# Normalised tiles of a hybrid decoder layer transposed by DMA instead of TensorE, with the first MLP norms taken before the mixer's end and the MLP weights loaded by one queue

## The chip, the cores and the metric

The kernel runs on the 8 cores of one Trainium2 chip. Each core works by itself on its share of the batch; nothing is exchanged. A core has five engines, each with its own instruction stream that runs in program order: TensorE (PE: matmuls, and transposes written as matmuls), VectorE (DVE), ScalarE (ACT), GpSimd (POOL) and SyncE (SP). PE writes to PSUM, eight banks of 128 x 512 float32; the other operands lie in SBUF. SP, ACT and POOL also issue DMA transfers, each in its own order. The metric is the device time of the slowest core, in microseconds (us).

## The reference

One layer of a decoder with adaptive norms: a token mixer (recurrence on half the width, short convolution on the other) and an MLP, each with a residual, then a final norm. Cut to what matters:

```python
D_MODEL = 1024; BATCH = 8; SEQ = 2048; DEC_BATCH = 128; DEC_SEQ = 8; H_REC = 4; D_FF = 4096

def hybrid_layer(x, c, s_rec, s_conv, lb, w_ada, b_ada, w_in, w_conv, g_onorm, w_out, w_up, w_down):
    mod = jax.nn.silu(c) @ w_ada + b_ada
    sh1, sc1, g1, sh2, sc2, g2 = jnp.split(mod[:, None, :], 6, axis=-1)
    h = rms_norm(x) * (1 + sc1) + sh1
    q, fz, i, g, gb, gc, hv = jnp.split(h @ w_in, SPLITS, axis=-1)
    logf = jnp.log(lb_h + (1.0 - lb_h) * jax.nn.sigmoid(fz32))
    k = (1.0 - lb_h) * jax.nn.sigmoid(-fz32)
    o_rec, s_rec_new = hgrn2_chunked(q, k, logf, i, s_rec)      # state 128 x 128 per head, in chunks
    o_rec = per_head_rms(o_rec) * g_onorm * jax.nn.silu(g)
    y_conv, s_conv_new = short_conv(gc * hv, s_conv, w_conv)
    mix = jnp.concatenate([o_rec, gb * y_conv], axis=-1) @ w_out
    x = x + g1 * mix
    h2 = rms_norm(x) * (1 + sc2) + sh2
    x = x + g2 * (jnp.square(jax.nn.relu(h2 @ w_up)) @ w_down)
    return x, s_rec_new, s_conv_new

def reference(...):        # one layer, for 8 prompts and for 128 samples with a state of their own
    ...
    y = rms_norm(x) * g_final
```

## The kernel before

**Work of a core.** One prompt of 2048 tokens, in 16 blocks of 128, and 16 sample sequences of 8 tokens, which make one more block. The mixer takes the prompt in eight tiles of two blocks, p0 to p7, with the sample tile s after p3: the order is p0, p1 (their steps interleaved), p2, p3, s, p4, p5, p6, p7. Then the MLP takes the 17 blocks in six groups: (sample, 0, 1), (2, 3, 4), (5, 6, 7), (8, 9, 10), (11, 12, 13), (14, 15).

**The order.** The program is written down as a list of operations with what they read and write. A planner takes the list with its place in it as priority and with a cost for each operation, and puts each engine's operations in a fixed order; semaphores are set by what depends on what. So an operation's place on its engine is decided before the run, and an engine stands at an instruction whose operand is not there.

**A norm.** `normed` loads a block x (128 tokens x 1024, ACT's queue) into one of two buffers `xn`, forms the sum of squares and the factor on ACT (Square, Ln, Exp), and DVE writes x times the factor as bf16 into one of two buffers, W0 and W1. The matmuls want the width on the partitions, so each block is transposed, in eight pieces of 128 x 128. PE does this (`tr`, L415) into a PSUM bank, M1 (ring `NR`); DVE reads the bank and writes scale and shift applied: `hT` for the mixer (`norm1`, eight passes of 128 x 256 a tile; two buffers, a third early), `h2T` for the MLP (`norm2`, eight passes of 128 x 128 a block). For the sample block, which has another scale and shift for each sequence, `sample_mod` does it with four tensor-tensor passes of 128 x 512.

**A mixer tile.** `mixer_tile` runs in steps: F (decays), V (values), Q (queries), G (gate), R (the recurrence, block by block: transpose of the keys `nk`, scores, masked scores `sm` times values, state products, each with the one bank M0, ring `MR`; then the norm of the output: square, a reduction by a matmul with ones into M0, Ln, Exp, a DVE product, two POOL products into `mix`), C, H and B (convolution, matmuls of `hT` with the blocks of w_in), and then the output projection (wout, banks U0 and U1) with the residual. `norm1` of the next tile stands in the list ahead of a tile's own steps. For the sample tile SP loads 16 states `Sl` and stores them back, in seven buffers.

**Around the MLP.** At step B of p7 the seven first loads of up weights (`wup`, SP's queue, out of a bf16 copy in DRAM, `wscr`) and `norm2` of the first group are listed. `h2T` lies over the buffers W6 to W8 that the steps up to B use, `wup` over w_in, `wdn` partly over what the mixer leaves; so each waits for the last use. Down weights go through POOL's queue, held back by `load_dn` until an up load has landed. Per group the list has `up` (256 matmuls of up to 384 columns for three blocks, square of relu into `uT`), `norm2` of the next group, `down` (192 matmuls of 512 columns, the second residual, final norm, store).

In the rows a name ends in a buffer number of the tool's own (`W_135`, `W_136` are W0, W1; `hT_60` to `hT_62` are hT0 to hT2). Helpers: matmul L404, transpose L415, activation L431, tensor-tensor L438, tensor-scalar L442 and L444, DMA L465.

Of the kernel before, what the change touches and what calls it, by code (L numbers as in the profile page):

```python
# [368 lines left out]
def build_program():  # L369
# [348 lines left out]
    def normed(src_d, rdeps):  # L718
        x, xn = xnR.take()
# [5 lines left out]
        return nbv, nbn  # L725

    def sample_mod(nbv, nbn, dst, dst_n, c0, j_sh, j_sc):
        M, Mn = NR.take()
        Mb = M[:, :].bitcast(BF16)
        tr([(Mb[:, j * 128:(j + 1) * 128], nbv[:, j * 128:(j + 1) * 128], ident) for j in range(8)], [nbn, "cB"], [Mn])  # L730
        for jh in range(2):
            W, Wn = WT.take()
# [484 lines left out]
```

How the kernel before makes its waits and increments, by code:

```python
            def run(e, h):  # L325
                for o in order[e]:
                    for key, (val, d) in need_of[o.idx].items():
                        if d.chan is not None:
                            h.wait_ge(csem[key], val * 16)
                        else:
                            h.wait_ge(esem[key], d.cnt)
                    ins = o.fn(h)
                    if o.chan is not None:
                        ins.then_inc(csem[o.chan], 16)
                    elif o.signal:
                        ins.then_inc(esem[e], 1)
                if e == "sp":
                    for c, n in self.chans.items():
                        h.wait_ge(csem[c], n * 16)
```

## Time and profile before

| | us |
|---|---|
| median of 3 runs (lowest to highest) | 929.19 (928.15 to 932.9) |
| the profiled execution | 927.96 |
| its span, slowest core (5) | 926.4 |
| busy: PE, DVE, ACT, POOL | 826.0, 466.9, 366.2, 166.8 |
| PE's share of the chain that ended last | 75% |

The profile is of one execution. A row of the stage view gives start and end of a stretch, its length, then for PE, PE's weight loads (PEld), DVE, ACT and POOL the time that the engine worked in it with the number of instructions, then the granted clock of PE as a share of full speed, the busy share of the 16 DMA engines, and GB/s. A row of a timeline gives start, duration, engine, line, operation, out<-in with shapes, how many like it follow one another, and in square brackets how long the engine stood before it and what released it. A row of the view by lines gives, behind the bar, busy time in all and mean ns of one, then the idle time before. A row of transfers gives queue, count, KB each and the median us from issue to landing. Matmuls are pipelined: the distance between two starts says more than a duration.

The run has three parts: about 75 us of loading and modulation, the mixer until 437, the MLP from 437 to 916.

### The profile page before, as it was taken

To read this page: it belongs to the slowest core of one execution; us is meant where nothing else is said; L and a number is where in the kernel's file an instruction comes from. 1 tells how busy PE (TensorE), PEld (TensorE's weight loads), DVE (VectorE), ACT (ScalarE), POOL (GpSimd) and SP (SyncE) were. 2 spreads that over 40 slices of the span, in tenths; PEclk is the share of its full clock that TensorE was granted. 3 is DMA by queue.
4 is the path that set the end of the run, shared out by engine and by line. 5 is a ranking of instruction groups with operands and counts; after the bars stand their busy time and mean duration, and the time that the engine had idled before them with its cause. 6 is when DMAs were issued, how large, how long until landed. Compare 5 with 4: busy or idle time off the path is not lost.

```text
span 926.4 us, 16715 instructions; the slowest of 8 cores (914.6 to 926.4 us)
## 1 busy us (share of the span) xinstructions
PE 826.0 (89%) x5929; PEld 513.6 (55%) x5929; DVE 466.9 (50%) x851; ACT 366.2 (40%) x780; POOL 166.8 (18%) x218
## 2 busy tenths in 40 slices
PE   0147999999898999986999999999999999999995
PEld 0124876777676657653654565456446545644862
DVE  0023597667879687685443445234514533442421
ACT  2036558374747567632330333133214312311411
POOL 2000022332153342242201200200120021002001
PEclk9997999999999999996999999999999999999998
DMA  8999789999346668798996211210221012002001
GB/s 161 215 183 196 137 161 162 201 181 235 112 149 239 140 174 201 188 241 187 227 195 157 95 43 47 91 69 2 91 69 46 24 46 91 2 1 83 31 2 45
DMA packets 27436, 113.93 MB, mean 123 GB/s; under 512 B 3845, under 2 KB 4229, under 8 KB 22362
## 3 DMA queue, kind: packets, MB, share of 16 engines
q0 software_dynamic: 4848, 39.19, 26.8%
q1 hardware_dynamic: 17610, 55.85, 18.9%
q10 hardware_dynamic: 4896, 17.83, 6.2%
q8 instruction: 48, 0.79, 0.3%
q14 instruction: 34, 0.28, 0.1%
HBM read 129.56 MB, written 30.88 MB: 173 GB/s over the span
## 4 chain that ended last, share of the span: by engine, by line
PE 75%; DVE 6%; DMA 6%; issue 6%; ACT 5%; ACTq 0%; POOL 0%; DVEq 0%; POOLq 0%
PE G L404 41%; PE U L404 23%; PE O L404 9%; DMA win_44<-w_in 5%; PE M L415 1%; DMA cB<-constB 1%; ACT W_140 L431 1%; DVE Sd_85 L438 1%; DVE h2T L444 1%; PE M L404 1%; DVE Ts_84 L438 1%; ACT Sb_86 L431 1%; ACT W_142 L431 0%; ACT W_141 L431 0%; ACT W_139 L431 0%
## 5 line engine op out<-in xcount | busy, mean ns | idle before, releaser
L444 DVE TENSOR_SCALAR h2T<-M,modT 128x128 bf16<-128x128 bf16 x128 | 43.9, 343 | 23.7 <-PE M L415 13.7
L431 ACT ACTIVATE W_140<-G 128x384 f32<-128x384 f32 (+2 forms) x38 | 19.7, 519 | 52.3 <-PE G L404 52.3
L415 PE MATMUL M<-cB,W_135 128*128 128x128 bf16 (+1 forms) x144 | 13.3, 231 | 30.1 <-DVE lnoml L438 20.9
L431 ACT ACTIVATE W_135<-xn_145 128x1024 bf16<-128x1024 f32 x17 | 17.9, 1053 | 45.6 <-PE M L415 36.2
L431 ACT ACTIVATE W_136<-xn_146 128x1024 bf16<-128x1024 f32 x17 | 17.9, 1053 | 25.7 <-PE M L415 15.8
L438 POOL TENSOR_TENSOR xr_147<-xr_147,W_138 128x512 f32<-128x512 f32 x8 | 10.5, 1312 | 97.1 <-DVE W_138 L438 96.9
L415 PEld LDWEIGHTS M<-cB,W_135 128*128 128x128 bf16 (+1 forms) x144 | 9.9, 104 | 32.6 <-issue 31.2
L431 ACT ACTIVATE Sb_86<-Sd_85 128x512 bf16<-128x512 f32 x16 | 10.0, 627 | 37.8 <-DVE Sd_85 L438 37.8
L438 POOL TENSOR_TENSOR xr_147<-xr_147,W_137 128x512 f32<-128x512 f32 x5 | 6.3, 1267 | 102.6 <-DVE W_137 L438 102.6
L438 DVE TENSOR_TENSOR uT<-W_138,G 128x384 bf16<-128x384 f32 (+1 forms) x26 | 13.7, 528 | 17.2 <-ACT W_138 L431 16.6
L404 PE MATMUL G<-hT_60,win_44 128*128 128x256 bf16 x128 | 18.4, 303 | 4.4 <-DMA win_44<-w_in 4.4
L431 ACT ACTIVATE W_137<-G 128x384 f32<-128x384 f32 (+1 forms) x24 | 11.4, 475 | 25.8 <-PE G L404 25.0
L438 DVE TENSOR_TENSOR Ts_84<-Sd_85,U 128x512 f32<-128x512 f32 x31 | 21.1, 682 | 0.7
L431 ACT ACTIVATE W_140<-W_140 128x512 f32<-128x512 f32 x32 | 20.1, 630 | 2.1
L404 PE MATMUL G<-wdn_129,uT 128*128 128x512 bf16 x88 | 20.8, 379 | 0.0
L404 PE MATMUL G<-wdn_128,uT 128*128 128x512 bf16 x88 | 20.8, 379 | 0.0
L404 PE MATMUL G<-wdn_127,uT 128*128 128x512 bf16 x88 | 20.8, 379 | 0.0
L404 PE MATMUL G<-wdn_130,uT 128*128 128x512 bf16 x88 | 20.8, 379 | 0.0
L438 DVE TENSOR_TENSOR uT<-W_137,G 128x384 bf16<-128x384 f32 (+1 forms) x24 | 12.9, 537 | 15.6 <-ACT W_137 L431 14.1
L431 ACT ACTIVATE W_138<-G 128x384 f32<-128x384 f32 (+1 forms) x26 | 12.2, 469 | 21.0 <-PE G L404 21.0
L438 DVE TENSOR_TENSOR uT<-W_139,G 128x384 bf16<-128x384 f32 (+1 forms) x24 | 13.0, 542 | 14.5 <-ACT W_139 L431 14.5
L438 DVE TENSOR_TENSOR W_138<-U,Gp 128x512 f32<-128x512 f32 x16 | 11.0, 687 | 16.3 <-PE U L404 15.0
(565 smaller groups left out, 2149.0 us busy)
## 6 DMA issues: line engine op xcount, KB each, us to landing
wscr<-w_up POOLq DMA_DIRECT2D x8, 1024.0 KB, 14.9
xn_146<-x ACTq DMA_DIRECT2D x9, 512.0 KB, 4.7
xn_145<-xp ACTq DMA_DIRECT2D x8, 512.0 KB, 11.0
xn_146<-xp ACTq DMA_DIRECT2D x8, 512.0 KB, 9.6
ada_111<-w_ada POOLq DMA_DIRECT2D x4, 1024.0 KB, 13.4
ada_112<-w_ada POOLq DMA_DIRECT2D x4, 1024.0 KB, 22.5
xn_145<-x ACTq DMA_DIRECT2D x8, 512.0 KB, 3.4
xr_148<-xp SPq DMA_DIRECT2D x6, 512.0 KB, 14.7
```

The costliest lines, as they stand in the source:

```text
L404: ins = e.matmul(o_, lhsT=l_, rhs=r_, start=st, stop=sp_, skip_group_check=True)
L415: ins = e.transpose(out=o_, in_=i_, identity=id_)
L431: return P.op("act", lambda e: e.activation(out=out, in_=in_, func=func, **kw), r, w, c, prio=prio)
L438: return P.op(eng, lambda e: e.tensor_tensor(out=out, in0=in0, in1=in1, op=op), r, w, vec_cost(eng, out, mode), prio=prio)
L444: f = lambda e: e.tensor_scalar(out=out, in0=in0, scalar1=s1, scalar2=s2, op0=op0, op1=op1)
```

## The change

- From the fourth prompt tile on (`ti > 2`), for the sample tile and for all MLP norms, the normalised block is transposed by a DMA from SP's queue (`turned`): out of W0 or W1 into the `xn` buffer that held x. These are 28 transfers of 256 KB. DVE reads SBUF then; `norm1` has 16 passes of 128 x 128 a tile in place of 8 of 128 x 256. Tiles p0 to p2 keep the transposes on PE.
- `NR` is gone; M0 and M1 both serve the recurrence, and the transposes of p0 to p2.
- The three norms of the first MLP group are listed at step C of p7, up to and with their transposes (the third into the gate buffer `Gs`); at step B `norm2` gets them and only writes `h2T`.
- Up weights load through POOL's queue, in front of the down weights, which no longer wait for an up load.
- Modulation of the second half and the gates move: from tile 2's step Q to its R, from 2's B to tile 3's F, from 3's Q to 3's R.

```diff
-    GA = BankRing(["G0", "G1", "G2"]); MR = BankRing(["M0"]); NR = BankRing(["M1"]); ...
+    GA = BankRing(["G0", "G1", "G2"]); MR = BankRing(["M0", "M1"]); ...
     def load_up(j):
-        up_ops[j] = dma("sp", flat(wup[j]), wscr_d[j], ["wscr%d" % j], [wup_n[j]], MB2 / 2)
+        up_ops[j] = dma("pool", flat(wup[j]), wscr_d[j], ["wscr%d" % j], [wup_n[j]], MB2 / 2)
     def load_dn(j):
-        gate = up_ops.get(4 if j == 2 else 7)
-        dma("pool", flat(wdn[j]), wdn_d[j], [], [wdn_n[j]], MB2, after=[gate] if gate else ())
+        dma("pool", flat(wdn[j]), wdn_d[j], [], [wdn_n[j]], MB2)
...
+    def turned(nb):
+        nbv, nbn, x, xn = nb
+        xt = x[:].bitcast(BF16)[:, 0:1024].rearrange("p (j t) -> p j t", t=128)
+        P.op("sp", lambda e: e.dma_start_transpose(xt, nbv.rearrange("p (j n) -> p j n", n=128)), [nbn], [xn], 1200.0, dma=300000.0)
+        return xt, xn
...
     def norm1(kind, ti):
+        if ti > 2:
+            for b in range(2):
+                xt, xn = turned(nbs[b])
+                for jj in range(8):
+                    ts("dve", h[:, jj, b * 128:(b + 1) * 128], xt[:, jj, :], modT[:, 8 + jj, 0:1], modT[:, jj, 0:1], ...)
+            return h, hn
         for jh in range(2):
-            M, Mn = NR.take()
+            M, Mn = MR.take()
...
-    def norm2(blocks):
+    def norm2(blocks, ready=None):
         for s, blk in enumerate(blocks):
-            nbv, nbn = normed(x1_d[blk], ["x1_%d" % blk])
+            xt, xn = ready[s] if ready else turned(normed(x1_d[blk], ["x1_%d" % blk]))
...
-            M, Mn = NR.take()
-            tr([(Mb[:, j * 128:(j + 1) * 128], nbv[:, j * 128:(j + 1) * 128], ident) for j in range(8)], [nbn, "cB"], [Mn])
...
+            if step == "C" and n_ + 1 == len(tiles):
+                n0 = [turned(normed(x1_d[b], ["x1_%d" % b], (Gs, "Gs") if i == 2 else None)) for i, b in enumerate(bgroups[0])]
             if step == "B" and n_ + 1 == len(tiles):
                 for j in UPORD[:7]:
                     load_up(j)
-                norm2(bgroups[0])
+                norm2(bgroups[0], n0)
```

PE at the end of tile p7, before; names here keep their buffer and bank (G1<-hT1_61 is bank G1 from buffer hT1, wout and mix are the output projection's):

```order
L404 MATMUL G1<-hT1_61,win4_47 128x256 x8
L415 MATMUL M1<-cB_156,W1_136 128x128 x8
L404 MATMUL M0<-sq1_91,cB_156 128x512
L415 MATMUL M0<-cB_156,nk3_70 128x128 x2
L415 MATMUL M0<-cB_156,nk0_67 128x128 x2
L404 MATMUL M0<-qd3_66,nk3_70 128x128 x2
L404 MATMUL M0<-qd0_63,nk0_67 128x128 x2
L404 MATMUL U0<-vt0_74,kt1_72 128x128 x4
L404 MATMUL U1<-vt0_74,kt1_72 128x128 x4
L404 MATMUL O0<-sm0_88,vt0_74 128x128 x4
L404 MATMUL O0<-qd3_66,Sb1_87 128x64 x2
L404 MATMUL O0<-qd0_63,Sb1_87 128x64 x2
```

The same place after:

```order
L404 MATMUL G0<-hT1_61,win4_47 128x256 x8
L404 MATMUL M0<-qd3_66,nk3_70 128x128 x2
L404 MATMUL M0<-qd0_63,nk0_67 128x128 x2
L404 MATMUL G0<-hT1_61,win4_47 128x256 x8
L404 MATMUL G1<-hT1_61,win4_47 128x256 x16
L404 MATMUL O0<-sm0_88,vt0_74 128x128 x4
L404 MATMUL O0<-qd3_66,Sb1_87 128x64 x2
L404 MATMUL O0<-qd0_63,Sb1_87 128x64 x2
L404 MATMUL O0<-qd3_66,Sb0_86 128x64 x2
L404 MATMUL O0<-qd0_63,Sb0_86 128x64 x2
L404 MATMUL M1<-sq0_90,cB_156 128x512
L404 MATMUL U0<-wout0_50,mix2_152 128x512 x8
```

The L415 transposes out of W1 and W0 are gone, the key transposes (`nk`) stand further up, and the scores (`qd` with `nk`) stand ahead of the last projection's matmuls (`win4`) instead of behind them.

PE from the first group's up stage (`wup`, the last block of columns) into its down stage (`wdn`), before:

```order
L404 MATMUL G<-h2T,wup_59 128x384 x16
L415 MATMUL M<-cB,W_135 128x128 x8
L404 MATMUL G<-wdn_127,uT 128x512 x8
L404 MATMUL U<-wdn_127,uT 128x512 x16
L415 MATMUL M<-cB,W_136 128x128 x8
L404 MATMUL G<-wdn_128,uT 128x512 x8
```

and after:

```order
L404 MATMUL G<-h2T,wup_59 128x384 x16
L404 MATMUL G<-wdn_127,uT 128x512 x8
L404 MATMUL U<-wdn_127,uT 128x512 x16
L404 MATMUL G<-wdn_128,uT 128x512 x8
L404 MATMUL U<-wdn_128,uT 128x512 x16
```

The transposes of the next group's norms, eight at a time, have gone from between the matmuls.

DVE in tile p4, where `hT1` of tile p5 is written (`Sl`, `km` are the sample states and their keys), before:

```order
L438 TENSOR_TENSOR ub0_92<-WX1_114,G1 128x16x8
L438 TENSOR_TENSOR Sd0_85<-Ts0_84,dec1_99 128x512
L444 TENSOR_SCALAR hT1_61<-M1,modT_154 128x256
L448 SCALAR_TENSOR_TENSOR W8_143<-ub0_92,vecT_104,W8_143 128x128
L444 TENSOR_SCALAR hT1_61<-M1,modT_154 128x256
L448 SCALAR_TENSOR_TENSOR W8_143<-ub0_92,vecT_104,W8_143 128x128
L444 TENSOR_SCALAR hT1_61<-M1,modT_154 128x256 x2
L448 SCALAR_TENSOR_TENSOR W8_143<-ub1_93,vecT_104,W8_143 128x128 x2
L438 TENSOR_TENSOR W4_139<-O0,W4_139 128x512
```

and after, where the scaling that this block's transpose needs, `L442 TENSOR_SCALAR W0_135<-xn0_145,st4_161 128x1024`, stands three rows ahead of the first of these:

```order
L438 TENSOR_TENSOR Sl0_118<-Sl0_118,U1 128x512
L448 SCALAR_TENSOR_TENSOR W8_143<-ub1_93,vecT_104,W8_143 128x128 x2
L438 TENSOR_TENSOR mix1_83<-G2,W8_143 128x4x128
L448 SCALAR_TENSOR_TENSOR sg1_79<-G0,vecT_104,W5_140 128x256
L442 TENSOR_SCALAR km1_126<-kt2_73,cF_155 128x512
L448 SCALAR_TENSOR_TENSOR sg1_79<-G0,vecT_104,W5_140 128x256
L438 TENSOR_TENSOR Sl2_120<-Sl2_120,U1 128x512
L452 SCALAR_TENSOR_TENSOR W8_143<-cB_156,WX3_116 128x512
L438 TENSOR_TENSOR Sl1_119<-Sl1_119,U0 128x512
L442 TENSOR_SCALAR km1_126<-kt2_73,cF_155 128x512
L438 TENSOR_TENSOR qd1_64<-G1,WX2_115 128x512
L444 TENSOR_SCALAR hT1_61<-xn0_145,modT_154 128x128 x2
```

Before, the pass reads the PSUM bank M1; now it reads xn0, which the DMA writes, and 13 rows stand between the scaling and the first pass.

## Rows read from the trace of the kernel before

**Rows 1.** The stages of core 5, columns as told above.

```profile
75.00:240.00 165.00, 158.86 (x1525) 118.51 (x1523) 110.04 (x195) 95.64 (x195) 35.60 (x60) 0.97 0.91 184
240.00:410.00 170.00, 155.57 (x1371) 111.47 (x1369) 135.01 (x227) 107.80 (x215) 65.04 (x85) 0.99 0.66 174
410.00:437.00 27.00, 16.41 (x101) 8.59 (x99) 17.48 (x35) 9.37 (x21) 7.30 (x8) 0.68 1.00 202
420.00:430.00 10.00, 4.21 (x16) 1.87 (x17) 6.21 (x17) 2.18 (x7) 2.11 (x3) 0.50 0.74 134
437.00:916.00 479.00, 477.53 (x2737) 262.80 (x2735) 188.74 (x368) 131.83 (x304) 48.74 (x41) 1.00 0.25 71
```

**Rows 2.** Timeline of PE between an up stage and a down stage.

```profile
562.64 1.46 PE L404 MATMUL U<-h2T,wup_59 128*128 128x384 bf16 x8
563.94 0.61 PE L415 MATMUL M<-cB,W_136 128*128 128x128 bf16 x8
564.38 1.89 PE L404 MATMUL U<-wdn_127,uT 128*128 128x512 bf16 x8
566.11 1.89 PE L404 MATMUL U<-wdn_128,uT 128*128 128x512 bf16 x8
```

**Rows 3.** Timeline of PE from the mixer's end to the MLP.

```profile
411.08 0.61 PE L415 MATMUL M<-cB,W_136 128*128 128x128 bf16 x8
...
417.86 1.01 PE L415 MATMUL M<-cB,W_135 128*128 128x128 bf16 x8 [0.66 <-DVE W_139 L438]
...
420.80 0.59 PE L404 MATMUL M<-sq_90,cB 128*128 128x512 bf16 x1 [1.25 <-ACT st_161 L431]
423.54 1.01 PE L415 MATMUL M<-cB,W_136 128*128 128x128 bf16 x8 [2.15 <-DVE h2T L444]
427.39 3.57 PE L404 MATMUL U<-wout_50,mix_152 128*128 128x512 bf16 x8 [2.83 <-POOL mix_152 L438]
...
437.02 3.25 PE L404 MATMUL G<-h2T,wup_53 128*128 128x384 bf16 x19
```

**Rows 4.** Timelines of ACT, DVE and POOL in the same stretch.

```profile
420.08 0.58 ACT L431 ACTIVATE sq_90<-O 128x512 bf16<-128x512 f32 x1
...
424.27 0.63 ACT L431 ACTIVATE W_137<-W_137 128x512 f32<-128x512 f32 x1 [2.19 <-DVE h2T L444]
...
425.01 0.69 DVE L438 TENSOR_TENSOR W_137<-O,W_137 128x512 f32<-128x512 f32 x1 [1.61 <-ACT W_137 L431]
...
426.52 0.72 POOL L438 TENSOR_TENSOR mix_152<-W_137,sg_78 128x256 bf16<-128x256 f32 x1
```

**Rows 5.** Groups by line: DVE's passes for the norms, and a tensor-tensor pass.

```profile
L444 DVE TENSOR_SCALAR h2T<-M,modT 128x128 bf16<-128x128 bf16 x128 | 43.9, 343 | 23.7 <-PE M L415 13.7
L438 DVE TENSOR_TENSOR Ts_84<-Sd_85,U 128x512 f32<-128x512 f32 x31 | 21.1, 682 | 0.7
...
L444 DVE TENSOR_SCALAR hT_60<-M,modT 128x256 bf16<-128x256 bf16 x32 | 13.1, 409 | 3.9 <-PE M L415 2.2
```

**Rows 6.** Timeline of DVE early on: a pass of 128 x 136 in SBUF.

```profile
47.22 0.23 DVE L442 TENSOR_SCALAR modT<-modT 128x136 f32<-128x136 f32 x1
```

**Rows 7.** Transfers: issue, count, KB each, median us to landing.

```profile
wdn_134<-w_down POOLq DMA_DIRECT2D x1, 1024.0 KB, 48.5
...
Sl_120<-srec SPq DMA_DIRECT2D x2, 256.0 KB, 8.8
...
recs<-Sl_124 SPq DMA_DIRECT2D x2, 256.0 KB, 3.6
...
recp<-rout SPq DMA_DIRECT2D x1, 256.0 KB, 21.9
```

**Rows 8.** Timeline of PE at the start: p1's first projection.

```profile
78.78 3.57 PE L404 MATMUL G<-hT_62,win_44 128*128 128x256 bf16 x16 [2.79 <-DVE hT_62 L444]
```

**Rows 9.** Timelines of DVE and PE: hT1 of p5 written, and first used.

```profile
251.80 0.41 DVE L444 TENSOR_SCALAR hT_61<-M,modT 128x256 bf16<-128x256 bf16 x1
...
281.26 1.91 PE L404 MATMUL G<-hT_61,win_44 128*128 128x256 bf16 x16
```

**Rows 10.** Timeline of POOL: the issue of the last down weights.

```profile
450.99 0.57 POOL L465 DMA_DIRECT2D wdn_134<-w_down  x1
```

More of the change, by code:

```diff
@@ L716, in rstd, with normed @@
         return s_, sn
-    def normed(src_d, rdeps):
-        x, xn = xnR.take()
+    def normed(src_d, rdeps, buf=None):
+        x, xn = buf or xnR.take()
         dma("act", x[:], src_d, rdeps, [xn], 128 * 4096)
@@ L737, in sample_mod @@
             shb = AP(modT, (j_sh + 4 * jh) * 17 + 1, [[544, 128], [17, 4], [1, 16], [0, 8]])
-            tt("dve", tmv, trv, scb, ALU.mult, [Mn, "modT"], [Wn])
+            tt("dve", tmv, trv, scb, ALU.mult, [xn, "modT"], [Wn])
             tt("dve", hv, tmv, shb, ALU.add, [Wn, "modT"], [dst_n])
@@ L1007, in mixer_tile @@
             dma("sp", x1_d[xblk + b], xr[:], [xrn], ["x1_%d" % (xblk + b)], 128 * 4096)
-    def norm2(blocks):
+    def norm2(blocks, ready=None):
         for s, blk in enumerate(blocks):
-            nbv, nbn = normed(x1_d[blk], ["x1_%d" % blk])
+            xt, xn = ready[s] if ready else turned(normed(x1_d[blk], ["x1_%d" % blk]))
             if blk == SAMPLE:
-                sample_mod(nbv, nbn, h2T, "h2T%d" % s, s * 128, 16, 24)
+                sample_mod(xt, xn, h2T, "h2T%d" % s, s * 128, 16, 24)
                 continue
-            M, Mn = NR.take()
-            Mb = M[:, :].bitcast(BF16)
-            tr([(Mb[:, j * 128:(j + 1) * 128], nbv[:, j * 128:(j + 1) * 128], ident) for j in range(8)], [nbn, "cB"], [Mn])
             for j in range(8):
-                ts("dve", h2T[:, j, s * 128:(s + 1) * 128], Mb[:, j * 128:(j + 1) * 128], modT[:, 24 + j, 0:1], modT[:, 16 + j, 0:1],
-                   ALU.mult, ALU.add, [Mn, "modT"], ["h2T%d" % s], mode=1.0)
+                ts("dve", h2T[:, j, s * 128:(s + 1) * 128], xt[:, j, :], modT[:, 24 + j, 0:1], modT[:, 16 + j, 0:1],
+                   ALU.mult, ALU.add, [xn, "modT"], ["h2T%d" % s], mode=4.0)
     def up(blocks):
@@ L1127, in build_program @@
         for step in gen(n_):
-            if n_ == 2 and step == "Q":
+            where = ("2R", "3F", "3R")
+            key = "%d%s" % (n_, step)
+            if key == where[0]:
                 late_mod(0)
                 load_ada(8); load_ada(9)
-            if n_ == 2 and step == "B":
+            if key == where[1]:
                 late_mod(1)
                 load_ada(10); load_ada(11)
-            if n_ == 3 and step == "Q":
+            if key == where[2]:
                 gates(1)
+            if step == "C" and n_ + 1 == len(tiles):
+                n0 = [turned(normed(x1_d[b], ["x1_%d" % b], (Gs, "Gs") if i == 2 else None)) for i, b in enumerate(bgroups[0])]
             if step == "B" and n_ + 1 == len(tiles):
```

15 lines of the change are left out of this document (8 added, 7 removed).

## The prediction, made before the changed kernel had run

> **What bounds the kernel now.** I read the span by stages first [rows 1]: what counts is how near TensorE (PE) comes to filling each. The MLP, 437 to 916 us, is PE from end to end: 477.53 of 479 us, DMA at 0.25. An instruction taken off PE there is time taken off the kernel. The mixer from 240 to 410 is less pure: PE works 155.57 of 170 us, VectorE (DVE) 135.01, so 14.4 us of PE time go to waits, and DVE, which works in program order, has 35 us to spare (busy share 0.79). The hole is 410 to 437: PE works 16.41 of 27 us, its granted clock is 0.68 (0.50 from 420 to 430), and the DMA share is 1.00. The PE timeline of that hole [rows 3] and the rows of the other engines beside it [rows 4] say what is in it: transposes of the first MLP norms (L415, out of W_136, W_135, W_136) in between the last steps of the recurrence, each of which waits for DVE; a reduction at 420.80; and the output projection only at 427.39, which waited 2.83 us for POOL's `mix`.
>
> **The change, part by part** (against the profiled execution: 927.96 us, span 926.4, so 1.56 us lie outside the span; the median of the runs is 929.19, 1.2 above it).
>
> *E, MLP norms.* Of the 17 norm blocks 14 lie between an up and a down stage. In the MLP eight transposes start at 563.94 and the next matmul at 564.38 [rows 2]: 0.45 us a block. Nothing else is on PE then, so 14 x 0.45 = **-6.3 us**. What replaces them must hide: load, norm, DMA transpose, eight DVE passes. A group's down stage is 24 groups of eight matmuls (1.73 us each, [rows 2]) = 41.5 us for three blocks. Two buffers of x serve three blocks, so the third block's load waits for the first's DVE passes; allow 8 us for that and 4 for the third's own norm and passes, and the cover still holds for a transpose of about 29 us.
>
> *D, the transition.* PE reaches 411.08 with its last projection done and starts the output projection at 427.39: 16.3 us [rows 3]. Only a little of that is the recurrence's work: four `kt` transposes, four scores and eight state products of 128 columns (16 x 0.056) and one reduction of 512 (1.73 / 8), 1.1 us on PE, which after the change stand ahead of the last projection's matmuls. What must follow the last projection is the output of the last chunk (about 1 us with its hand-over) and a chain [rows 4]: square 0.58, reduction 0.59, Ln (taken as the Exp) 0.63, Exp 0.63, DVE 0.69, two on POOL 2 x 0.72, and five hand-overs of about 0.13 (from 420.80 plus 0.59 and from 426.52 plus 0.72 to the next start): 5.2 us. So 16.3 - (1.0 + 5.2 + 1.1) = 9.0 us saved. In the trace the chain was held by the norms: Exp at 424.27 stood behind a DVE pass of `h2T` [rows 4]. The output projection, too, took 9.63 us (427.39 to 437.02), where four groups of its kind at full clock take 4 x 1.73 = 6.9; the clock had fallen in the hole before. The hole gets shorter but stays; I take half of 2.7: -1.4. The three norms themselves now run earlier, at step C, with three loads, three squares on ACT and three scalings on DVE, into a stage where DVE has 0.21 to spare. The writing of `h2T` must still wait for step B (the space is shared); it is 16 passes and four sample passes (0.23 and 0.68, by [rows 5, 6]), about 6 us, and hides under chain and projection (13 us). D = -9.0 - 1.4 = **-10.4 us** (bounds -6 and -13: all of the norms' 2.8 us of DVE and ACT on the path and no clock back, or the full clock back and the hand-over nil).
>
> *B, mixer tiles.* For the sample tile and tiles p3 to p7, 11 blocks of eight transposes leave PE: 11 x 0.45 = 4.9 us. Between nothing (if PE only waits longer) and all of it I take 0.6, below PE's share of 0.92, since some stand before waits: **-3.0 us**. DVE: the eight passes of 128x256 out of PSUM, 0.409 each, 3.3 us a tile [rows 5], become 16 of 128x128 out of SBUF. No such row exists; nearest are 0.343 (the same size out of PSUM, [rows 5]) and 0.23 (128x136 in SBUF, float32, [rows 6]). By 0.23 that is 3.7 us a tile, by 0.343 5.5: 0.4 to 2.2 us more on DVE a tile, in its spare time; it costs nothing or, over five tiles, 11 us if DVE were the bound. I take 0, by the SBUF row and because h is done early: p5's last pass ran at 251.80 and PE first used it at 281.26 [rows 9]. In the MLP and the hole the same passes get cheaper for DVE, which doesn't matter there.
>
> *C, the wait added.* DVE meets a tile's passes in its fixed order; if the transpose has not landed, everything behind stands: the scans, the scores' masks, the states of the sample tile, and PE behind these. In the new order the closest distances from a norm's scaling to its first pass are 13 rows of that order (second blocks of p4 and p5), 17 (both of p6), 22 or more for the rest. At 0.68 a row [rows 5] and a busy share of 0.79, 13 are 11.2 us and 17 are 14.6 us. The transpose moves 256 KB. Nearest rows [rows 7]: 256 KB transfers of the same queue and stage take 3.6 to 8.8 us; one of 256 KB issued in the hole took 21.9. I take 6, from the first two, since the transposes are issued where these run. Then C = **0**. SP also issues in order, and the second block of p5 stands behind four reloads of sample states that wait for stores; I leave that in the range (+3).
>
> *A, start.* Tiles p0 to p2 keep PE transposes, now through two banks that the recurrence shares. p1's h was waited for 2.79 us [rows 8], and its transposes no longer stand behind `kt`; on the other side a transpose of p2 now stands ahead of the first use of p1's h. I take **-1** (-4 to +3). The later gates and modulation keep the same work: 0.
>
> *Loads.* All up and down weights now go through POOL's queue. wdn_134 was issued at 451 [rows 10] and took 48.5 [rows 7], so it landed near 499.5; it was first needed near 515 (437, an up stage of 32 x 1.30, then 7/8 of the down's 41.5), and 13 us sooner, near 502, by B and D. I price this at 0.
>
> Sum: -6.3 - 10.4 - 3.0 - 1.0 = -20.7, so 927.96 - 20.7, **about 907 us**. Own range: 898 to 916.
>
> The trace has the eight PE transposes at 56 ns each [rows 2]. The Trainium skill ("VectorE: DVE Perf Modes", The three transpose paths) gives a 128x128 bf16 transpose 390 ns on TensorE and 1309 ns through the DMA's crossbar, and its Rules for kernel authors say to use TensorE where PSUM will do as the destination. The row is far under the page's TensorE figure, and no row here shows the DMA's. By the page a block would take 8 x 1.309 = 10.5 us, an estimate just inside the 11.2 above, and the sum would stand; with the wait in the queue on top it would fall under the second rival.
>
> **The rivals.**
> 1. *The hole stays.* With the norms gone, the tail hangs on DVE and ACT (state update, `Sb`, mask), which have their own three norms to do just before. For it: DVE at 0.79, and 1.25 and 2.83 us of the PE waits in the hole [rows 3] were for ACT and POOL. Against it: the Exp row [rows 4]. Then D is -3, B -1.5, A 0: -10.8, **917 us**.
> 2. *Slower: the transposes land late and DVE stands.* Mechanism C with a transpose of T us: 2 x (T - 11.2) + 2 x (T - 14.6) us are lost in the mixer, all on the path while PE has no other tile's matmuls left. The loss equals the gain of 20.7 at T = 18. At the 21.9 of [rows 7], 36 us and a few more from the blocks at 22 rows: 928 - 21 + 36 = 943; at 20, **936 us**. For it: SP's queue has the states' stores and reloads ahead, and no transpose row exists. Against it: the rows at 3.6 to 8.8.
> 3. *The first MLP starves.* One queue for 16 loads of 1 MB: `wup` come behind each other, and the hole had a DMA share of 1.00 already [rows 1]. If the last loads land 10 us later than before, near 510 where 502 is wanted, 8 are lost: **916 us**; it also takes POOL's time for issuing, beside `mix`.
> 4. *Better.* The two banks let scores and `kt` run ahead, and a third of the 14.4 us of PE waits goes, with the full clock in the projection: -27, **900 us** or a little under.
>
> **How the numbers follow.** Forecast 0.50; rival 1 0.18; rival 3 0.10; rival 2 0.14; rival 4 0.08. About 0.5% (4.6 us) is what a measurement of this kernel can tell from no change, so faster is below 924.5, slower above 933.8. The forecast, rival 4 and most of rivals 1 and 3 are faster: 0.77. What is left of these, and the mild end of rival 2, is same: 0.10. Slower is rival 2's rest: 0.13. The range leaves out rival 2 (0.14) and the far end of rival 4: 895 to 928.
>
> **What would show it.** E: no L415 between up and down, and the next up some 1.35 us sooner per group of three. D: the gap on PE between the last projection and the output projection near 7.5 us instead of 16.3, its clock above 0.50, `h2T` passes after the gated multiply. B, C: DVE's waits by releaser: none, or few, on the transposes; a landing time of 4 to 9 us. If DVE waits on them, with PE waiting for DVE in 240 to 410, rival 2 holds. Rival 3: PE waiting for a wup or wdn load between 425 and 510. The forecast is wrong at once if the transposes take more than about 15 us each, or if the stage 240 to 410 gets longer.

## The result, and the profile after

The changed kernel takes 972.12 us (median of 4 runs, 968.68 to 972.4) where the kernel before takes 929.77 (4 runs beside it): 1.0443 times as long, with an interval of 1.0406 to 1.0479. The forecast was 907, the range 895 to 928. It is slower by 42 us, and the sign is wrong.

Ratios, here and below, compare undisturbed runs alone. The profiled execution took 971.97 us. Its cores, each with its span and the mean granted clock of PE:

```profile
core 0: 915.7 us, clock 0.980
core 1: 949.0 us, clock 0.958
core 2: 930.7 us, clock 0.971
core 3: 926.4 us, clock 0.972
core 4: 954.2 us, clock 0.962
core 5: 970.1 us, clock 0.951
core 6: 937.8 us, clock 0.971
core 7: 918.0 us, clock 0.976
```

In the kernel before all eight lay between 914.6 and 926.4. So there are two things to explain: why cores 0 and 7 gain only 3.7 us each (from 919.4 and 921.7), and why the others lose up to 44. The work is the same on all eight, and in the other three executions other cores lead and trail: core 1 is the fastest in one, with 918.8 us, and the slowest in the other two, with 970.4 and 970.5. Which core loses is no property of the core.

Stages of core 5 after (columns as in [rows 1]; the third stretch is the hole before the MLP, the last two are pieces of the first):

```profile
75.00:240.00 165.00, 117.69 (x1007) 82.61 (x1006) 84.16 (x146) 73.97 (x146) 30.14 (x49) 0.87 0.98 133
240.00:465.00 225.00, 195.50 (x1747) 142.03 (x1746) 170.07 (x305) 130.59 (x263) 74.68 (x101) 0.95 0.78 177
467.00:488.00 21.00, 13.94 (x81) 7.52 (x80) 16.39 (x37) 3.64 (x7) 7.10 (x9) 0.84 1.01 239
488.00:968.00 480.00, 470.65 (x2623) 256.20 (x2620) 187.02 (x370) 134.19 (x316) 50.47 (x44) 1.00 0.33 83
140.00:150.00 10.00, 0.00 (x0) 0.00 (x0) 0.00 (x0) 0.00 (x0) 0.00 (x0) 0.50 1.70 69
...
95.00:110.00 15.00, 14.88 (x140) 11.73 (x139) 9.17 (x21) 9.20 (x21) 0.72 (x2) 1.00 1.06 174
```

Between 75 and 240 PE does 1007 matmuls where it did 1525 [rows 1]. Between 140 and 150 no engine executes anything, while the DMA engines are busy and move 69 GB/s (the share above 1 counts overlapping packets). The PE timeline names the hole:

```profile
128.45 0.49 PE L404 MATMUL G<-hT_61,win_44 128*128 128x256 bf16 x3 [0.52 <-DVE mix_83 L438]
166.31 1.25 PE L404 MATMUL G<-hT_61,win_44 128*128 128x256 bf16 x5 [37.36 <-issue]
```

PE stood 37.36 us in the middle of a group of eight equal matmuls, with nothing that the profile shows as its releaser. SP's queue on the same core just before (start, duration of the issue, transfer):

```profile
101.23 1.62 SPq L730 DMA_TRANSPOSE xn_145<-W_135  x1
102.96 23.47 SPq L730 DMA_TRANSPOSE xn_146<-W_136  x1
126.52 0.47 SPq L465 DMA_DIRECT2D gates<-xr_149  x1
175.37 0.34 SPq L465 DMA_DIRECT2D Gp<-gates  x1
```

These are the two blocks of p3, the first tile that goes by DMA. Issuing the second alone held SP for 23.47 us. The DMA view of 110 to 160 us shows what they do to the core's other transfers. First core 5 (queue: packets, MB, share of 16 engines; then transfers with the median us from issue to landing):

```profile
q1 hardware_dynamic: 1822, 0.45, 74.5%
q0 software_dynamic: 274, 1.95, 45.2%
q14 instruction: 1, 0.01, 0.0%
...
ada_112<-w_ada POOLq DMA_DIRECT2D x1, 1024.0 KB, 57.4
wout_51<-w_out POOLq DMA_DIRECT2D x1, 1024.0 KB, 53.4
...
xn_146<-W_136 SPq DMA_TRANSPOSE x1, 63.7
```

Then core 0, in the same 50 us of the same run:

```profile
q1 hardware_dynamic: 2241, 2.25, 32.2%
q8 instruction: 4, 0.07, 0.5%
...
ada_112<-w_ada POOLq DMA_DIRECT2D x1, 1024.0 KB, 9.7
wout_51<-w_out POOLq DMA_DIRECT2D x1, 1024.0 KB, 10.0
...
xn_146<-W_136 SPq DMA_TRANSPOSE x1, 14.8
```

The hardware queue of core 5 moved 0.45 MB in 1822 packets (1858 packets of all kinds were under 512 bytes) and held the 16 engines for 74.5% of the window. Weight loads that took 10 us on core 0 took 53 to 57. Queue q8, of the kind "instruction", has four packets on core 0 and none on core 5. Cores 4, 5 and 6 agree in this: q8, which has a packet of 16 KB every 10 to 20 us in the kernel before, has none there between some 108 us and 152.5, 164.0 and 146.3 us, and on each of them PE goes on 2.2 to 2.3 us after that late packet. So it looks as if PE's stand was for its own instructions, stuck in the same crowd. That rests on these rows, and was not tried alone.

The other cores follow the same pair of transfers, if not strictly. Landing time of p3's second block, and the mixer from p0's first projection matmul to the end of p7's last (before: 349.8 to 355.6 us, 352.7 in the mean):

| core | 0 | 7 | 3 | 2 | 1 | 6 | 4 | 5 |
|---|---|---|---|---|---|---|---|---|
| landing, us | 14.8 | 18.8 | 18.4 | 18.7 | 28.3 | 45.0 | 51.7 | 63.7 |
| mixer, us | 364.3 | 364.9 | 375.1 | 375.0 | 397.5 | 388.2 | 394.7 | 418.2 |

Core 1 stands out of this order because of a second late block, p6's second. It was issued into a stretch with the DMA share at 0.99 (318 to 352 us) and landed after 30.7 us; DVE stood for it before p6's passes:

```profile
319.62 1.27 SPq L730 DMA_TRANSPOSE xn_145<-W_135  x1
350.37 2.43 DVE L444 TENSOR_SCALAR hT_60<-xn_145,modT 128x128 bf16<-128x128 bf16 x6 [15.55 <-DMA xn_145<-W_135]
```

On cores 3 and 5 the same block took 22.9 and 25.1 us, and DVE stood 8.73 and 10.23 us for it; on the other five cores it took 9.4 to 11.7 us. DVE waited as well for the gate of the prompt, `Gp`: 8.2, 7.0 and 8.7 us on cores 4, 5 and 6.

The parts that were to gain did gain. The MLP takes 482.0 or 482.1 us on five of the eight cores (489.3 or 489.4 before on six), and between up and down there is nothing on PE, against [rows 2]:

```profile
611.41 1.46 PE L404 MATMUL U<-h2T,wup_59 128*128 128x384 bf16 x8
612.71 1.89 PE L404 MATMUL U<-wdn_127,uT 128*128 128x512 bf16 x8
```

The transition on core 5's PE, against [rows 3]:

```profile
467.58 2.78 PE L404 MATMUL G<-hT_61,win_47 128*128 128x256 bf16 x24
470.20 0.39 PE L404 MATMUL O<-sm_88,vt_74 128*128 128x128 bf16 x4
...
472.69 0.38 PE L404 MATMUL M<-sq_90,cB 128*128 128x512 bf16 x1 [1.86 <-ACT sq_90 L431]
478.26 3.57 PE L404 MATMUL U<-wout_50,mix_152 128*128 128x512 bf16 x8 [5.20 <-POOL mix_152 L438]
...
487.54 1.63 PE L404 MATMUL G<-h2T,wup_53 128*128 128x384 bf16 x9
```

From the end of the last projection (PE's next instruction starts at 470.20) to the output projection it is now 8.1 us, 8.0 to 8.2 over the cores (before 15.2 to 16.3). The L415 rows are gone from it; what PE waits for is the square, and then POOL's `mix`.

### The profile page after: what moved, and what is told of

Same layout as the page of the kernel before. It is cut to its first block, busy times and chain, and to the rows that moved or that the text cites. A ratio compares the mean times of both kernels' runs of the same rounds, so it can differ in the third digit from the quotient of the medians.

```text
span 970.1 us, 16398 instructions; the slowest of 8 cores (915.7 to 970.1 us)
## 1 busy us (share of the span) xinstructions
PE 821.9 (85%) x5705; PEld 506.0 (52%) x5705; DVE 475.0 (49%) x891; ACT 366.0 (38%) x780; POOL 172.3 (18%) x226
## 3 DMA queue, kind: packets, MB, share of 16 engines
q1 hardware_dynamic: 46026, 54.80, 25.5%
## 4 chain that ended last, share of the span: by engine, by line
PE 62%; DMA 16%; DVE 8%; issue 6%; ACT 3%; SPq 3%; POOL 1%; DVEq 0%; POOLq 0%; ACTq 0%
PE G L404 33%; PE U L404 21%; PE O L404 8%; DMA gates<-xr_149 5%; DMA win_44<-w_in 4%; DMA xn_145<-W_135 3%; SPq L730 3%; DMA wscr<-w_up 3%; DMA Gp<-gates 1%; DVE hT_61 L444 1%; DMA cB<-constB 1%; DVE hT_60 L444 1%; DVE W_143 L448 1%; ACT W_140 L431 1%; ACT W_142 L431 1%
## 5 line engine op out<-in xcount | busy, mean ns | idle before, releaser
L431 ACT ACTIVATE W_140<-G 128x384 f32<-128x384 f32 (+2 forms) x38 | 19.7, 519 | 85.2 <-PE G L404 66.9
L404 PE MATMUL G<-hT_61,win_44 128*128 128x256 bf16 (+1 forms) x128 | 15.7, 272 | 39.2 <-issue 37.4
L404 PEld LDWEIGHTS G<-hT_61,win_44 128*128 128x128 bf16 x128 | 11.3, 102 | 42.2 <-issue 40.3
L415 PE MATMUL M<-cB,W_135 128*128 128x128 bf16 (+1 forms) x32 | 3.4, 261 | 31.4 <-DVE lnoml L438 18.9
L431 ACT ACTIVATE W_137<-G 128x384 f32<-128x384 f32 (+1 forms) x24 | 11.4, 476 | 45.9 <-PE G L404 25.8
L438 DVE TENSOR_TENSOR sm_88<-M,cB 128x512 bf16<-128x512 f32 x9 | 6.1, 680 | 37.9 <-PE M L404 37.9
L431 ACT ACTIVATE W_135<-xn_146 128x1024 bf16<-128x1024 f32 x7 | 7.4, 1059 | 45.7 <-DVE h2T L444 28.3
L438 DVE TENSOR_TENSOR uT<-W_137,G 128x384 bf16<-128x384 f32 (+1 forms) x24 | 12.9, 537 | 22.2 <-ACT W_137 L431 20.8
L444 DVE TENSOR_SCALAR h2T<-xn_145,modT 128x128 bf16<-128x128 bf16 x64 | 22.4, 350 | 2.4 <-PE U L404 0.2
L404 PE MATMUL U<-wout_50,mix_82 128*128 128x512 bf16 x48 | 13.0, 419 | 10.3 <-DVE W_138 L438 7.6
L431 ACT ACTIVATE W_136<-xn_145 128x1024 bf16<-128x1024 f32 x7 | 7.4, 1056 | 37.0 <-DMA xn_145<-x 36.9
L431 ACT ACTIVATE W_142<-G 128x512 f32<-128x512 f32 x10 | 5.8, 584 | 40.8 <-PE G L404 40.8
## 6 DMA issues: line engine op xcount, KB each, us to landing
wscr<-w_up POOLq DMA_DIRECT2D x8, 1024.0 KB, 11.9
xn_145<-xp ACTq DMA_DIRECT2D x8, 512.0 KB, 10.4
```

The lines of the kernel that those rows point to most:

```text
L404: ins = e.matmul(o_, lhsT=l_, rhs=r_, start=st, stop=sp_, skip_group_check=True)
L415: ins = e.transpose(out=o_, in_=i_, identity=id_)
L431: return P.op("act", lambda e: e.activation(out=out, in_=in_, func=func, **kw), r, w, c, prio=prio)
L438: return P.op(eng, lambda e: e.tensor_tensor(out=out, in0=in0, in1=in1, op=op), r, w, vec_cost(eng, out, mode), prio=prio)
L444: f = lambda e: e.tensor_scalar(out=out, in0=in0, scalar1=s1, scalar2=s2, op0=op0, op1=op1)
```

## The experiments

Three theories stand in the expectations: S, that DMA transposes issued while the DMA engines are full are what costs; V, that the short DVE passes of 128 x 128 cost; O, that the moved gates, the shared banks or the single queue cost. The runs e1 to e4, e5 to e8 and e9 to e12 each had the kernel before run beside them, which took 930.16, 930.75 and 927.06 us; across these groups ratios are compared, not times.

**e1_mlp_only**: the mixer's tiles and the sample block go back to PE; the MLP norms and all else stay as changed.

```diff
-        if ti > 2:
+        if ti > 7:
...
-            xt, xn = turned(normed(xs_d[:, :], []))
+            tr([(Mb[:, j * 128:(j + 1) * 128], nb[0][:, j * 128:(j + 1) * 128], ident) for j in range(8)], [nb[1], "cB"], [Mn])
```

> All mixer tiles, the sample tile too, go back to transposes on TensorE (two banks); MLP norms stay with the DMA, the first three held ready. Theory S (DMA transposes in the stage of full DMA starve TensorE of instructions on some cores, and the slowest core counts) and theory V (80 short VectorE passes out of SBUF slow the mixer on every core) both expect the mixer of before with the shorter transition and MLP: 929 - 7.4 - 6.4, some 912 to 918 us, cores within 12 us of each other. Theory O (the two banks, the moved gates and the one queue slow the mixer by themselves) expects 935 us or more.

929.09 us, 0.9988 of before (0.9976 to 1.0). The loss goes with the mixer's transposes, which speaks for S or V; but the time is not as low as they have it, so something in the rest costs as well. It has two places. The mixer is 360.1 us in the mean of the cores (352.7 before): on all eight, DVE waits 8.7 to 14.5 us once for the gate of the prompt, where it waited 0 to 3.5 before. On core 1:

```profile
154.18 0.69 DVE L438 TENSOR_TENSOR W<-U,Gp 128x512 f32<-128x512 f32 x1 [14.54 <-DMA Gp<-gates]
```

Its load was issued at 134.18, 2.4 us later than before (131.83), so it is mainly DVE that gets there sooner. And the second MLP group is late (e6).

**e2_p3_by_pe**: only p3 goes back to PE (`if ti > 3`).

> Only tile p3 goes back to TensorE; the sample tile, p4 to p7 and the MLP stay with the DMA. Theory S expects the TensorE stalls without a releaser between 100 and 170 us to go and the slowest core to come within some 15 us of the fastest: 920 to 937 us. Theory V expects only about 3 us: 965 us or more, with the cores still 30 us and more apart.

943.61 us, 1.0149 (1.0121 to 1.0177): of the 42 us, some 28 hang on the two blocks of one tile. The spread goes with them: the mixer takes 373.4 to 381.5 us on all cores, and no core's PE stands more than 1.3 us with no releaser. What stays above before is e1's gate wait (9.0 to 14.9 us on all cores), the passes (e4, e12) and transposes that are still late: one mixer block on each core, issued at 347 to 356 us, took 10.5 to 28.9 us to land, and the first transpose of the second MLP group held SP for 36.1 to 51.8 us (MLP 490.5 to 497.0 us). How the rest divides among these was not run apart.

**e3_two_unread**: the kernel before, with two added transposes of p3's blocks that nobody reads. They stand where the change has them, and write into the x buffers; PE still makes the tile.

```diff
+        if ti == 3:
+            for (nbv, nbn), (x, xn) in zip(nbs, ((last_x[2], last_x[3]), (last_x[0], last_x[1]))):
+                xt = x[:].bitcast(BF16)[:, 0:1024].rearrange("p (j t) -> p j t", t=128)
+                P.op("sp", lambda e, nbv=nbv, xt=xt: e.dma_start_transpose(xt, nbv.rearrange("p (j n) -> p j n", n=128)), [nbn], [xn], 1200.0, dma=300000.0)
```

> The kernel before with two more DMA transposes, of p3's two normalised blocks into the buffers of x; nobody reads them, TensorE still transposes, VectorE's passes are as before. Theory S expects stalls of TensorE without a releaser, 10 to 40 us, on some cores between 100 and 170 us, a late gates transfer there, and 935 to 975 us. Theory V expects no change: 927 to 932 us.

945.66 us, 1.0168 (1.0149 to 1.0186): two transfers of 256 KB whose result is not used cost 16 us. No pass, bank or gate is changed here, so S needs neither V nor O. But the way is not the one that S expected: PE never stands more than 1.8 us without a releaser, and DVE at most 1.0 us for the gate. So this run does not show that a transpose takes PE's instructions; what a late one holds up depends on what stands behind it. Here that is visible on core 1. The transfers took 32.4 and 39.0 us to land (35.7 in the mean); the next load of x into the same buffer, on ACT's queue, has to wait for that, and ACT's work stands behind it (ACT, and ACT's queue):

```profile
116.60 0.63 ACT L431 ACTIVATE W<-W 128x512 f32<-128x512 f32 x1
137.52 0.34 ACTq L465 DMA_DIRECT2D xn<-xs  x1
137.96 0.63 ACT L431 ACTIVATE Sb<-Sd 128x512 bf16<-128x512 f32 x1 [20.73 <-DMA xn<-W]
```

Over the cores, sorted by that landing time (10.3, 12.6, 20.9, 21.6, 25.7, 32.8, 35.6, 35.7 us) the mixer takes 354.5, 356.7, 368.1, 364.7, 374.1, 376.7, 374.3 and 385.1 us: about one for one.

**e4_plain_copy**: each transpose is a plain copy of the same 256 KB, in the same place of the same queue.

```diff
-        P.op("sp", lambda e: e.dma_start_transpose(xt, nbv.rearrange("p (j n) -> p j n", n=128)), ...)
+        P.op("sp", lambda e: e.dma_start(out=xt, in_=nbv.rearrange("p (j n) -> p j n", n=128)), ...)
```

> The changed kernel with each DMA transpose replaced by a plain copy of the same 256 KB from the same to the same buffer, so blocks are not turned; order, waits and passes are those of the changed kernel. Theory S with the many small packets of a transpose as its cause expects no starved core: 918 to 926 us, cores within 12 us. If the amount or the place in the queue were the cause, it stays at 960 to 975. Theory V expects the mixer from p0's to p7's first projection to stay some 15 to 20 us longer than before on every core, since the passes stay.

930.12 us, 1.0001 (0.998 to 1.0023). The turning by itself is 42 us; bytes, queue, waits and order are not. All cores agree (915.5 to 923.6), and the MLP is 482.0 us on each: that is the change without its trouble, and it still gains nothing, since the mixer is 367.5 us in the mean, 7.4 above e1 (on single cores 362.9 to 372.2, where cores 0 and 7 of the change lie as well). What lies between e1 and e4 is the passes out of SBUF and the copies, but not these alone: DVE waits 0 to 6.3 us for the gate in e4, less than in e1. Issuing a copy took SP about 0.5 us nearly everywhere. In the second MLP group, among the weight loads, the copies landed as late as the transposes do (49 to 51 us) and cost PE nothing; there the turning shows in SP's queue, which a transpose holds for 21 to 47 us. DVE's groups of that shape, on core 0 (busy, mean ns, then idle before):

```profile
L444 DVE TENSOR_SCALAR hT<-xn,modT 128x128 bf16<-128x128 bf16 x80 | 30.5, 382 | 5.3 <-DVE hT L444 0.2
L444 DVE TENSOR_SCALAR hT<-M,modT 128x256 bf16<-128x256 bf16 x24 | 9.8, 407 | 2.0 <-DVE hT L444 0.5
```

80 passes take 30.5 us where 40 at 0.407 took 16.3: 14 us more on DVE. In the changed kernel itself, also core 0, the same passes vary with the buffer:

```profile
L444 DVE TENSOR_SCALAR hT_60<-xn_145,modT 128x128 bf16<-128x128 bf16 x24 | 10.6, 443 | 1.5
L444 DVE TENSOR_SCALAR hT_60<-xn_146,modT 128x128 bf16<-128x128 bf16 x24 | 7.5, 312 | 2.0 <-DVE hT_60 L444 0.2
```

**e12_narrow_passes** puts a price on them alone: the kernel before, PE transposes and all, but p4 to p7 read PSUM in 16 passes of 128 x 128.

```diff
+                if ti > 3:
+                    for b in range(2):
+                        ts("dve", h[:, jj, b * 128:(b + 1) * 128], Mb[:, j * 256 + b * 128:j * 256 + (b + 1) * 128], ...)
+                    continue
```

> The kernel before, where tiles p4 to p7 have 16 VectorE passes of 128 x 128 out of PSUM and not 8 of 128 x 256; no DMA transpose anywhere. VectorE does 16 x 0.343 - 8 x 0.409 = 2.2 us more a tile, 8.9 in all. Theory V expects most of that in the mixer: 933 to 938 us. If VectorE has room, it stays at 928 to 931.

931.73 us, 1.0069 (1.0043 to 1.0094): +6.4 us for four tiles (5.3 in the mixer of the profiled execution). 64 of these passes took 21.8 us, the 32 wide ones that are left (p0 to p3) 13.1, at the 409 ns of [rows 5]:

```profile
L444 DVE TENSOR_SCALAR hT<-M,modT 128x128 bf16<-128x128 bf16 x64 | 21.8, 341 | 3.3 <-PE M L415 0.9
L444 DVE TENSOR_SCALAR hT<-M,modT 128x256 bf16<-128x256 bf16 x32 | 13.1, 409 | 6.8 <-PE M L415 4.8 <-DVE hT L444 0.5
```

Of 8.7 us added to DVE 6.4 came through to the end (4.0 to 8.7 by the interval), in tiles whose stage has DVE busy 0.79 of the time [rows 1]. So V holds as well, at about a sixth of the 42 us that e4 gives to S.

**e5_wide_passes**: e2, with both blocks of a tile turned into one buffer, so that DVE has 8 passes of 128 x 256 again.

```diff
-                xt, xn = turned(nbs[b])
-                for jj in range(8):
-                    ts("dve", h[:, jj, b * 128:(b + 1) * 128], xt[:, jj, :], ...)
+            xt, xn = turned2(nbs)
+            for jj in range(8):
+                ts("dve", h[:, jj, :], xt[:, jj, :], ...)
```

> As e2 (p3 by TensorE), but the DMA turns both blocks of a tile p4 to p7 into one buffer, so VectorE reads SBUF in 8 passes of 128 x 256 a tile and not in 16 of 128 x 128. Theory V (the short passes slow the mixer) expects some 2.5 us less a tile on VectorE and 931 to 938 us against e2's 943.6; if the passes are hidden, it stays at 940 to 947.

959.79 us, 1.0299 (1.0246 to 1.0352), slower than e2. The mixer does fall, from 377.3 to 370.7 us in the mean: 6.6. But the time from the start of the output projection to the MLP grew from 8 to 10 us to between 18.6 and 33: DVE stands 8.9 to 22.5 us for the third of the first MLP norms (`Gs`), whose transpose took 25.5 to 39.2 us to land. It speaks on V through its mixer alone, and for it.

**e6_first_norms_early**: e1, with the first MLP group's norms listed at step F of p7 in place of C.

```diff
-            if step == "C" and n_ + 1 == len(tiles):
+            if step == "F" and n_ + 1 == len(tiles):
```

> As e1 (all mixer tiles by TensorE), but the three first MLP norms, with their DMA transposes, are listed at step F of p7 and not at C, ahead of the up loads. If e1's 8.5 us wait of TensorE for h2T at the MLP's start is a transpose that landed late among the up loads, it goes and the MLP falls from 490 to 482 us: 920 to 923 us. If it is the writing of h2T after step B that is late, nothing changes: 927 to 931.

930.2 us, 0.9991 (0.9972 to 1.001): no change from e1. The delay is not in the first group but in the second, whose transposes are issued while the weights load. Core 0, SP's queue:

```profile
443.00 45.54 SPq L730 DMA_TRANSPOSE xn<-W  x1
...
489.60 9.38 SPq L730 DMA_TRANSPOSE xn<-W  x1
```

and PE at the end of the first group's down stage:

```profile
522.28 2.72 PE L404 MATMUL G<-h2T,wup 128*128 128x384 bf16 x8 [6.65 <-DVE h2T L444]
```

**e11_e6_second_group_by_pe** takes that away: e6 with the second group's blocks transposed by PE.

> As e6 (two banks, one queue), but the second group's norms by TensorE. Expected by the same theory: the 6.7 us wait of TensorE for h2T at the second group goes, 1.4 us of transposes come back: 923 to 926 against e6's 930. If it waits for weights instead, 928 or more.

922.31 us, 0.9967 (0.9946 to 0.9988). By the ratios that is some 2 us under e6, and the intervals overlap; what the edit does is clear in the MLP, which takes 484.6 to 485.2 us (489.6 to 491.9 on seven cores of e6) although PE does three more blocks. DVE's wait for the gate stays (10.4 to 14.6 us on all eight).

**e7_early_old_banks** and **e8_early_old_two_queues** go after O. e7 is e6 with the recurrence on M0, the norms on M1, and modulation and gates at their old places; e8 also has the up loads on SP's queue and the down loads held back again.

```diff
-    GA = BankRing(["G0", "G1", "G2"]); MR = BankRing(["M0", "M1"]); ...
+    GA = BankRing(["G0", "G1", "G2"]); MR = BankRing(["M0"]); NR = BankRing(["M1"]); ...
```

> As e6, but one bank for the recurrence and one for the norms, and gates and modulation at their old places. Theory O (banks and moved gates cost the mixer the 5 us that e1 lost there) expects 4 to 6 us less than e6; otherwise within 2 us of e6.

> As e7, with the up loads back on SP's queue and the down loads held back as before, so that of the change only the MLP norms by DMA and the early first norms are left. If one queue starves the first MLP, this is faster than e7 by 3 us or more; if it is neutral, within 2 us of e7; a transpose behind the up loads on SP would make it slower by 5 to 10 us.

e7: 937.38 us, 1.0071 (1.0041 to 1.0101). The mixer is as before (351.0 to 355.6 us), and DVE's gate wait is 1.8 to 4.5 us on all eight; so O is right on most of the 7.4 us that e1's mixer is too long (e6's mixer, with the same norms early, is 358.6 in the mean, e7's 353.5), and which of the two parts does it, the banks or the moved places, was not run apart. The whole is slower, since PE waits in the MLP that starts earlier: 2.6 to 5.9 us for up weights on all cores, and on four of them another 5.5 to 13.1 us for `uT`, which goes back over ACT and POOL to a block of the residual (`xr`) that SP loads among the weights. On cores 4 and 5 the late one is the first group's third transpose. e8: ratio 1.0 (0.9963 to 1.0038), with single executions from 926.59 to 967.6 us; these lie too far apart to tell whether two queues give anything back.

**e9_late_groups** and **e10_late_groups_first_early** keep what worked. e9 is the kernel before, with DMA transposes only for the 11 blocks of the third to sixth MLP group, when the weights are in. e10 adds the first group's three norms at step F of p7.

```diff
+            elif blocks in bgroups[:2]:
+                tr([(Mb[:, j * 128:(j + 1) * 128], nb[0][:, j * 128:(j + 1) * 128], ident) for j in range(8)], [nb[1], "cB"], [xn])
+            else:
+                xt, xn = turned(normed(x1_d[blk], ["x1_%d" % blk]))
```

> The kernel before with one thing from the change: the norms of the MLP's third to sixth group (11 blocks) are transposed by DMA, when the loads of the weights are over and the DMA share is about 0.25. The theory that a DMA transpose is cheap where the DMA is idle and dear where it is full expects 11 x 0.45 us less on TensorE and no wait for a transpose: 5 us less than before, 923 to 926 us. If a DMA transpose does harm in itself, it is 928 or more.

> As e9, and the three first norms by DMA at step F of p7 (as e8, but the second group by TensorE, so no transpose is issued while the weights load). If the second group's transposes, stuck 45 us and more behind the weight loads, cost e6 to e8 their gain, this falls below e9, to 915 to 921. If the earlier MLP only waits for its weights instead, it is 923 to 930.

e9: 924.2 us, 0.9973 (0.9956 to 0.999). e10: 920.24 us, 0.994 (0.9917 to 0.9963), the fastest here: 5.6 us under the kernel before by the ratio, and some 47 under the change. On core 5 of e10 the third group's transposes pass SP in these rows (of the last two, the first):

```profile
481.51 10.47 SPq L731 DMA_TRANSPOSE xn<-W  x1
...
500.15 1.67 SPq L731 DMA_TRANSPOSE xn<-W  x1
...
568.46 3.34 SPq L731 DMA_TRANSPOSE xn<-W  x2
```

The first still holds SP for 10.47 us and lands after 21.3, with the DMA share at 1.32 (480 to 492 us); the next two take about 1.7 us each. None makes PE wait: its only waits in the MLP, in us and times, are for the second group's blocks and for `mix`:

```profile
PE M L415 <- DVE h2T L444: 1.3, 2, 1.0
PE U L404 <- POOL mix L438: 1.2, 1, 1.2
```

## Why the prediction was wrong, point by point

- **E, MLP norms: right.** -6.3 forecast; 489.4 to 482.0, so -7.4, on the five cores that have no wait in the MLP. On these the cover held; it broke on cores 2 and 4 and in e1, e2 and e6, where the second group's transposes were issued among the weight loads and landed too late for PE.
- **D, the transition: right in kind, 2 to 3 us too large.** -10.4 forecast: -9.0 for the gap and -1.4 for the clock. The norms did leave the chain, and the gap fell from 16.3 to 8.1 us on core 5, where 7.5 was written. The clock gave nothing back in the mean: the output projection took 9.0 us before and 8.8 after (core 5: 9.63 and 9.28), since the hole that is left still lowers it (0.84 in the stage view). Together -8.6 on core 5, -7.7 on core 0, between the bounds.
- **A and the banks: wrong sign.** -1 forecast, the later gates priced at 0. e1 has the mixer 7.4 us longer, e7 gives most of it back: in e1 DVE reaches the prompt's gate 8.7 to 14.5 us before it is there. "The later gates and modulation keep the same work: 0" is the failed sentence; the work is the same, its deadline isn't.
- **B, mixer tiles: mis-sized, and its zero fell.** -3.0 for PE and 0 for DVE. The pass was taken at 0.23 by the row of another pass, in float32; it measures 0.31 to 0.47. The upper bound (11 us if DVE were the bound) was the nearer one: +7.4 in the mixer from e1 to e4, +6.4 in e12. A busy share of 0.79 [rows 1] was read as spare time; but PE and DVE hand work to each other all along, and some three quarters of what e12 put on DVE came out at the end. "h is done early" [rows 9] didn't help, because what is late is not h but what stands behind its passes.
- **C, the wait: this step turned the sign.** It is where the prediction failed: one landing time of 6 us, taken from loads of the same stage [rows 7] against 21.9 from the hole, was put on all the mixer's transposes, and so C became 0. For most blocks 6 was near: from the sample tile to p7, without p6's second, the changed kernel's transposes landed in 3.0 to 13.1 us, median 5.0. For p6's second block it was 9.4 to 30.7. The first pair, though, is issued at 101 to 107 us, in a stretch with the DMA share at 1.06 (95 to 110 us above; 0.92 and 0.98 there on cores 5 and 0 of the kernel before). There even plain copies took 10.0 to 16.8 us (e4), and the transposes 11.6 to 63.7, so that the prediction's own sign of a wrong step ("more than about 15 us each") was met. The forecast looked only at the blocks with the fewest rows between scaling and passes, p4 to p6; p3 was among the rest. And its sum had no place for what a slow transpose does beside being late: it holds SP (23.47 us), the gates and weights land late, and PE stands (37.36 us).
- **Rival 2 named the kind, and its way was the smaller part.** It had the transposes land late and DVE stand, slower from T = 18, chance 0.14. That happened for one block: p6's second, on cores 1, 3 and 5. There the landing time less DVE's stand is 15.1, 14.2 and 14.9 us, so the prediction's 14.6 us of cover was right. The larger losses went round it: the queue that issues is held, gates and weights crawl behind, and PE stands without a releaser (37.36 us of core 5's loss; 25.0 on core 4, 19.7 on core 6, 11.9 on core 1, at most 2.5 elsewhere). Why PE stood stays open. The price 2 x (T - 11.2) + 2 x (T - 14.6) gave 36 us at 21.9, close to what was seen, by luck: of its four blocks one was late.
- **Rival 3 didn't happen** in the changed kernel: five cores have no wait in the MLP at all. Cores 2 and 4 lost 4.8 and 9.1 us there.

Put together for core 0, by its own rows before and after: start of p0 +1.4, mixer +10.0 (354.3 to 364.3), gap and projection -7.7, MLP -7.3, in all -3.6; its span fell by 3.7. The same for core 5: start -6.6, mixer +65.7 (352.6 to 418.2), gap and projection -8.6, MLP -6.8, in all +43.7, by which its span grew. Of the 65.7 PE's stand is 37.4, DVE's waits for p6's block and for the gate 10.2 and 7.0.

The step to doubt was the choice of 6 between rows at 3.6 and 21.9. It went by the sort of transfer, and the stage view beside it said otherwise: the first transposes were to go out in the stretch with the DMA at 0.91, not in the one with 0.66 [rows 1]. The Trainium skill's rule ("VectorE: DVE Perf Modes", Rules for kernel authors), TensorE wherever PSUM will do as the destination, is borne out by e2 and e11 where the DMA is crowded; in the quiet MLP, e9 gained by going against it.

## What to carry to other kernels

Before a transpose goes from an engine to a DMA queue, look up the DMA share at the very place where it is issued, not that of the stage; where it is near 1, the transfer, its queue and the loads beside it can all slow down by several times. A share near 1 is a warning, not a measure: other transposes of the changed kernel met one and landed in 4 to 10 us. Put such transfers where the DMA is quiet (here the MLP after its weights), and hold those of crowded stages on PE. And an engine with a fifth of its time free was no free engine here, where it alternates with the bound one: price such work nearer to all of it than to nothing (0.74 of it in e12, the one run that priced it alone).

## What the runs showed of the hardware

- DMA transposes and plain copies of 256 KB came near each other only where the DMA is quiet: in the MLP from 560 to 800 us mostly 3.0 to 3.1 us turned (the changed kernel) and 2.3 plain (e4). In the stretch where p3's go out a copy took up to 16.8 us and a transpose up to 63.7, with the hardware queue busy over 74.5% of 16 engines to move 0.45 MB in 1822 packets. The Trainium skill ("Advanced Engine Details and Errata", X-Bar Transpose) says that they are as fast as regular DMAs; the quiet figures come within about a third of that, but e3 (+16 us for two of them) and e4 (42 us less for the same bytes unturned) do not.
- Eight cores with the same program differed by 54 us in span, for the most part by how late one pair of transfers landed and what stood behind it.
- The `tensor_scalar` pass of 128 x 128 bf16 gained little from SBUF: 0.304 to 0.312 us in the best groups, 0.443 to 0.466 in others, 0.341 to 0.343 out of PSUM. What sets the difference between the groups was not tried.
- Issuing a transpose of 256 KB held SP's queue for 1.2 to 2.1 us in the quiet MLP of the changed kernel and for up to 51.8 us among the weight loads (e2); a plain copy held it for about 0.5 us in either place (e4).
- PE stood 37.36 us with all operands there, as far as the profile shows, while the instruction queue q8 had no packet, and went on 2.2 us after the next one; this was seen only in the changed kernel.
